# Moving small VectorE work inside the expert loops, two exponentials and one PSUM copy of a two-block transformer kernel

## What is computed

```python
def moe_ffn(tok, router_w, router_b, w1, w3, w2):
    ...
    for e in range(N_EXPERTS):                 # 16 experts, two of them chosen per token
        hid = jax.nn.silu(tok @ w1[e]) * (tok @ w3[e])
        out = out + gate[:, e:e + 1] * (hid @ w2[e])
    return out

def gla_chunk_scan(q, k, v, log_f):            # called for two directions, 8 heads
    ...
    b = jnp.cumsum(gc, axis=3)
    q_t = qc * jnp.exp(b)
    k_t = kc * jnp.exp(-b)
    ...

def dilated_window_attention(q, k, v, bias_table, window, dilation):
    ...
    m = jnp.max(s, axis=-1, keepdims=True)
    p = jnp.exp(s - m)
    ...
    o = jnp.einsum('bnqrhd,bnkrhd->bnqrhd', p, vh) / den[..., None]
```

## Time and profile before

| | us |
|---|---|
| three runs | 1763.42, 1764.65, 1765.15 |
| median | 1764.65 |
| the profiled execution, its own time | 1761.54 |
| its span in the trace | 1759.7 |
| PE busy, share of the span | 95% |
| DVE busy | 66% |
| ACT busy | 57% |
| share of PE in the chain that ended last | 80% |
| mean granted clock of TensorE | 0.988 |

### The profile page before, as it was taken

How to read it: one execution, slowest core, us unless ns; L and a number is a source line. 1 busy time by engine, 2 the same in 40 slices (tenths; PEclk the granted TensorE clock), 3 DMA queues, 4 the chain that set the end, 5 groups by cost and what they waited for, 6 DMA issues and landing times.

```text
span 1759.7 us, 30091 instructions
## 1 busy us (share of the span) xinstructions
PE 1679.4 (95%) x12246; PEld 1436.6 (82%) x12246; DVE 1154.5 (66%) x1595; ACT 1007.2 (57%) x1334; POOL 69.5 (4%) x66
## 2 busy tenths in 40 slices
PE   6999989899999989999999799999989999999898
PEld 4787666889888868889889688888869998897688
DVE  5332864789999874343465788989865677544564
ACT  4322753578888875224353678888854572453462
POOL 0000000000000110000000000000000000100100
PEclk9999999999999999999999899999999999999999
DMA  8646205899999954223574499999954443363512
GB/s 337 213 127 253 111 25 219 303 383 405 407 405 400 395 208 180 96 95 127 214 283 160 173 380 408 400 407 407 384 217 180 167 180 146 93 220 144 156 61 72
DMA packets 52556, 419.78 MB, mean 239 GB/s; under 512 B 16980, under 2 KB 18132, under 8 KB 30048
## 3 DMA queue, kind: packets, MB, share of 16 engines
q1 hardware_dynamic: 26416, 364.55, 52.6%
q0 software_dynamic: 8304, 31.64, 6.1%
q10 hardware_dynamic: 17728, 22.02, 3.7%
HBM read 398.22 MB, written 19.97 MB: 238 GB/s over the span
## 4 chain that ended last, share of the span: by engine, by line
PE 80%; DVE 8%; DMA 5%; ACT 4%; issue 3%; POOL 1%; SPq 0%; DVEq 0%; ACTq 0%; POOLq 0%
PE ps L755 47%; PE ps L900 17%; PE ps L716 4%; DMA ring<-w_all 3%; PE ps L739 2%; PE ps L909 1%; DMA y_d<-arena 1%; DVE w_lo L2314 1%; PE ps L1143 1%; PE ps L1154 1%; PE ps L1428 1%; PE ps L1169 1%; PE ps L916 1%; PE ps L762 1%; DMA arena<-y_d,tok_row 1%
## 5 line engine op out<-in xcount | busy, mean ns | idle before, releaser
L2314 DVE TENSOR_TENSOR w_lo<-ring,w_hi 128x1024 fp32r<-128x1024 f32 x384 | 452.4, 1219 | 50.8 <-ACT w_hi L1653 49.2
L1653 ACT ACTIVATE w_hi<-ring 128x1024 fp32r<-128x1024 f32 x384 | 395.7, 1056 | 106.9 <-PE ps L900 62.9
L755 PE MATMUL ps<-XT_lo,arena_r 128*128 128x256 f32 (+1 forms) x1712 | 384.6, 299 | 5.2 <-DVE ring_r L2166 3.9
L755 PEld LDWEIGHTS ps<-XT_lo,arena_r 128*128 128x128 f32 x1712 | 281.4, 189 | 21.0 <-issue 7.9
L900 PE MATMUL ps<-w_hi,x_hi 128*128 128x256 f32 (+1 forms) x768 | 250.1, 326 | 7.6 <-DVE w_lo L2314 4.8
L900 PE MATMUL ps<-w_lo,x_hi 128*128 128x256 f32 (+1 forms) x768 | 245.8, 320 | 0.0
L900 PE MATMUL ps<-w_hi,x_lo 128*128 128x256 f32 (+1 forms) x768 | 245.8, 320 | 0.0
L755 PE MATMUL ps<-arena_r 128*128 128x512 f32 (+1 forms) x656 | 230.6, 360 | 7.0 <-DVE arena_r L2486 3.7
L2166 DVE TENSOR_TENSOR ring_r<-ring,arena_r 128x1024 fp32r<-128x1024 f32 x96 | 114.0, 1222 | 108.4 <-ACT arena_r L1553 108.1
L755 PE MATMUL ps<-XT_lo,ring_r 128*128 128x256 f32 x640 | 180.9, 283 | 0.0
L900 PEld LDWEIGHTS ps<-w_hi,x_hi 128*128 128x128 f32 x768 | 147.2, 192 | 26.2 <-issue 8.9
(11 more groups left out here) (372 smaller groups left out, 2659.9 us busy)
## 6 DMA issues: line engine op xcount, KB each, us to landing
ring<-w_all SPq DMA_DIRECT2D x172, 2048.0 KB, 9.7
y_d<-arena ACTq DMA_DIRECT2D x30, 512.0 KB, 10.0
arena<-toep_d POOLq DMA_DIRECT2D x16, 384.0 KB, 12.1
arena<-rpb ACTq DMA_DIRECT2D x16, 192.0 KB, 3.8
xtok_d<-arena ACTq DMA_DIRECT2D x6, 512.0 KB, 3.2
hT<-h SPq DMA_DIRECT2D x2, 1024.0 KB, 6.1
arena<-cb_d POOLq DMA_DIRECT2D x1, 1536.0 KB, 12.0
arena<-cc_d POOLq DMA_DIRECT2D x1, 959.0 KB, 6.0
```

The lines of the kernel that those rows point to most:

```text
L755: last = nc.tensor.matmul(out, a, b, start=(first and i == 0), stop=(final and i == 2))
L1653: nc.scalar.activation(w_hi[:, q], slot(b, "p (q c) -> p q c", q=4)[:, q], ACT.Copy).then_inc(hi_rdy, 1)
L2314: nc.vector.tensor_tensor(w_lo[:, q], slot(base + n, "p (q c) -> p q c", q=4)[:, q], as_f32(w_hi[:, q]), ALU.subtract).then_inc(*split_sig ...
```

## The change

Three edits, and PE's program is left as it is. In `routed` on DVE, `weights_of_rows` becomes three functions with the same 20 instructions: `two_rows` (6 instructions) stands in turn 1 behind `gate_half` 0, `rows_taken` (6) in turn 1 ahead of `hidden_lo` 1, and `gates_taken` (8) in turn 14 ahead of `copy_rows(15)`; nothing is left behind `split(1, 0)`. On ACT, the first direction's exponentials move from step 12 to step 11; the second direction's stay in step 13. In the attention, the first copy out of PSUM moves from step 3, ahead of the exponentials of piece 3, to step 2, ahead of those of piece 2, and the two `last_split` move ahead of the exponentials of piece 1.

```diff
-                if u in (12, 13):
-                    act.wait_ge(b_rdy, u - 11)
-                    nc.scalar.activation(lf[:, u - 12], bc[:, u - 12], ACT.Exp)
-                    nc.scalar.activation(bc[:, u - 12], bc[:, u - 12], ACT.Exp, scale=-1.0).then_inc(e_rdy, 1)
+                if u in (11, 13):
+                    d = (u - 11) // 2
+                    act.wait_ge(b_rdy, d + 1)
+                    nc.scalar.activation(lf[:, d], bc[:, d], ACT.Exp)
+                    nc.scalar.activation(bc[:, d], bc[:, d], ACT.Exp, scale=-1.0).then_inc(e_rdy, 1)
...
             for i in range(len(AT_PAIRS) + 2):
-                if i >= 3:
+                if i == 1:
+                    last_split(0)
+                    last_split(1)
+                if i >= 4:
                     act.wait_ge(sx_t, AT0 + i - 2)
-                    if i >= 4:
-                        act.wait_ge(sx_o, AT0 + i - 3)
+                    act.wait_ge(sx_o, AT0 + i - 3)
+                    nc.scalar.activation(probsT2, ps[:, 4:7, :].rearrange("p b k -> p (b k)"), ACT.Copy).then_inc(sx_c, 1)
+                if i == 2:
+                    act.wait_ge(sx_t, AT0 + 1)
                     nc.scalar.activation(probsT2, ps[:, 4:7, :].rearrange("p b k -> p (b k)"), ACT.Copy).then_inc(sx_c, 1)
                 if 1 <= i < len(AT_PAIRS):
                     at_exp(i)
-                if 1 <= i < 3:
-                    last_split(i - 1)
...
-                def weights_of_rows():
+                def two_rows():
...
                     link(nc.vector.tensor_tensor(rsum, rsum, rmax, ALU.subtract))
+
+                def rows_taken():
+
                     link(nc.vector.tensor_tensor(kept, rsum, before_last, ALU.mult))
...
                     nc.vector.tensor_scalar(tok_row[:, 0:nt], rmax, -1.0, None, ALU.add)
+
+                def gates_taken():
+
                     link(nc.vector.tensor_tensor(tmp, top, gates, ALU.mult))
...
                     gate_half(e, j, 0)
+                    if first and j == 1:
+                        two_rows()
                     split(e, 2, (0, 1))
                     hidden_lo(e, 0)
                     gate_half(e, j, 1)
                     split(e, 2, (2,))
                     if begin:
                         tokens(2, 2, EXPERTS)
+                    if first and j == 1:
+                        rows_taken()
                     hidden_lo(e, 1)
                     split(e, 2, (3,))
+                    if not first and not last_e and isinstance(e, int):
+                        gates_taken()
                     if not last_e:
                         copy_rows(e + 1, 1 - j)
                         split(e + 1, 0, range(4))
-                    if begin:
-                        weights_of_rows()
```

## The result

| | before | changed |
|---|---|---|
| median of six runs, us | 1764.90 | 1753.43 |
| lowest, highest | 1761.64, 1765.81 | 1750.83, 1757.27 |
| ratio | | 0.9942 (95%: 0.9930 to 0.9954) |
| ratio, measured a second time | | 0.9951 (0.9937 to 0.9965) |
| profiled execution, us; span | 1761.54; 1759.7 | 1755.12; 1753.3 |

The change is faster by 0.58%, by 0.49% in the second measurement: 8.6 to 10.2 us. The forecast was 11.8.

What follows compares the result with a forecast made beforehand. PE is busy nearly all of the span, so only its waits and low clock can be won: 3.1 + 2.8 (experts) + 4.4 (recurrence) + 1.5 (attention) = 11.8 us, from the median 1764.65 to 1752.9 us; range 1749.0 to 1760.5.

Steps and rivals of the forecast that it cites:

- the first rival: The clock falls all the same, at remaining waits or the new 0.90; gain 6.5 us, time 1758.2 us; chance 0.10.
- the slow stretches vanish with the waits: Turn 1 of both expert layers and unit 16: low clock, twice 1.88 and 1.54, 5.3 us, goes with the waits.
- Turn 1, removal: Experts: PE's wait ahead of V and the slow V go whole, 4.17 us in layer 0, 3.7 in layer 1.
- clock term: The 5.3 us of low clock in the sum; without it the gain is 6.5 instead of 11.8 us.
- The new wait: Turn 1, layer 0: `two_rows` takes 1.28 us against 0.38 of slack, so PE waits 0.90 us.
- the experts' two terms: Net gains of the experts' edit: 3.1 us in layer 0 and 2.8 us in layer 1.
- `gates_taken` at nothing: Experts, turns 14 and 15: PE starts turn 15 about 0.5 us late, costed at nothing because DMA landings cover it.
- Recurrence: Units 14 to 16: the 2.82 us wait and 1.54 of low clock go, about 0.2 less 0.15 returns; 4.4 us gained.
- Attention: Product 0 comes 2.5 us sooner, later pieces gain 1.7 (even) or 1.1 (odd); 1.5 us taken.
- The weight stream: Rival: weight DMA bounds the expert loops, both layers give nothing; gain 5.9 us, time 1758.8 us; chance 0.12.
- The late third block: Rival: in every expert loop turn the third weight block lands late, PE waits 1.3 us; net 1784 us; chance 0.04.

Runs made afterwards that it cites:

- part_experts: The kernel before with only the experts' edit (the three functions in the experts' turns); ratio to before 0.9979, 3.7 us less.
- part_recurrence: The kernel before with only the recurrence's edit (first direction's exponentials in step 11); ratio to before 0.9978, 3.9 us less.
- part_attention: The kernel before with only the attention's edit (first copy and the two `last_split` moved); ratio to before 0.9988, 2.1 us less.
- attention_copy: The kernel before with the attention's first copy moved to step 2, the two `last_split` left where they were; ratios to before 1.0000 and 0.9996.
- idle_places: The changed kernel with `two_rows` ahead of `split(1, 1)` in turn 1, `gates_taken` ahead of `split(15, 1)` in turn 15; ratios to before 0.9927 and 0.9936.
- second_copy: The kernel of idle_places with the attention's copy of piece 1 also moved, ahead of the exponentials of piece 3; ratio to before 0.9941.

## Why the prediction was right, and where it was not

**The total** lies inside the range and goes the way that was forecast. The medians, 1753.4 for 1752.9, agree better than the gains do, 8.6 to 10.2 us for 11.8, and that closeness is luck. The range also took in the first rival (1758.2), so only the parts can decide between the two. What the waits cost was read rightly in sum. The sum was 1.6 to 3.2 us too large, most likely by what it booked for the clock.

**The step that was too large: the slow stretches vanish with the waits.** The text took 5.3 of its 11.8 us from it, twice 1.88 and 1.54. Counted over all thirteen profiles, by the granted clock of each microsecond:

| slow stretch | wait there | wait taken away |
|---|---|---|
| layer 0, V of turn 1 (359) | 3 of 6 | 0 of 7 |
| layer 0, D of turn 0 (346) | 2 of 6 | 5 of 7 |
| layer 1, V of turn 1 (1022) | 2 of 6 | 0 of 7 |
| clock lost from 285 to 372 (layer 0), us | 5.1 to 6.8, mean 5.7 | 3.4 to 6.8, mean 5.4 |
| clock lost around 965 to 1028 (layer 1), us | 6.8 in each | 5.1 to 8.5, mean 6.6 |
| unit 16 (1431) | 3 of 6 | 0 of 7 |
| last projections (1727 to 1737) | 0 of 4 | 6 of 9 |

The last row counts by the attention's edit, the ones above by that of the experts or of the recurrence. At the three places of the forecast a wait of 1.8 to 2.8 us is followed by the low clock in 8 of 18 cases, and where the wait is gone it never falls there (0 of 21). But around turn 1 of either layer what no longer falls in turn 1 falls nearby, in these profiles. Only at unit 16 is a part won on the spot: from the recurrence's first matmuls (1311.79 in the profile of before) to the start of unit 22 (1474.59), the six profiles with the wait take 161.3 to 164.0 us, mean 162.4, and the seven without it all 158.2. Of these 4.2 us, 3.1 are the wait (161.3 is the value at full clock) and 1.1 the clock.

Thirteen profiles are few, and their mean granted clocks mislead: it is 0.988 in both first profiles. But every timed run has a granted clock of its own. Span times (1 - clock) is the clock lost in that run, in us:

| kernel | runs | clock lost, mean us | less than before, us (95%) |
|---|---|---|---|
| before, all rounds | 63 | 24.6 | |
| changed, both measurements | 12 | 19.4 | 5.2 (3.5 to 6.9) |
| part_experts | 11 | 21.9 | 2.8 (1.3 to 4.2) |
| part_recurrence | 12 | 23.5 | 1.2 (-0.7 to 3.1) |
| part_attention | 12 | 23.2 | 1.5 (-0.4 to 3.3) |
| attention_copy, both | 24 | 26.2 | -1.6 (-3.0 to -0.1) |
| idle_places, both | 12 | 20.0 | 4.7 (3.0 to 6.3) |
| second_copy | 5 | 22.1 | 2.6 (1.0 to 4.1) |

So the change does take low clock away, and about as much as the 5.3 us of the forecast (5.1 in the round in which the two kernels ran side by side). But a lost us isn't a us of time everywhere: the attention's stretch takes 68.9 us with a slow stretch of 1.7 in it and 68.7 with none in the two profiles of idle_places, 69.7 and 68.6 in those of attention_copy. Among the runs of one kernel (151 runs, each against the mean of its kernel in its round) the time rises by 0.60 us for each us of clock lost. By that, an estimate, the clock gave 3.1 us where the forecast had 5.3. The means of the same runs lie 10.0 us apart, so 6.9 are left for all else. Which stretches went is not resolved, except that the experts' edit has a share.

The prediction had as its first rival that none of the low clock would go, with a chance of 0.10, and neither it nor the forecast's full 5.3 is what came. The rule that it set beside it, that the clock gate's windows run free of the kernel (the Trainium skill, "TensorE: Matmul & The Clock Gate", Part 1: The HAM clock gate), agrees with the traces: one and the same wait was followed by either level, and one kernel profiled twice had its stretches at 330 and 347 once and at 319 and 346 the other time. The error was to take one profile's coincidence of wait and clock for the full price of each wait. The 1.88 itself was also a little large: from U of turn 1 to U of turn 2 a slow stretch costs 1.6 us (21.96 for 20.33) in layer 0 and 1.5 (21.54 for 20.06) in layer 1.

Point by point:

- **Turn 1, removal.** The wait of 2.29 us went whole and V had no new one, as forecast. At full clock, from U of turn 1 to U of turn 2, it is 20.33 us before (part_attention: 352.40 to 372.73), 19.03 in the changed kernel (354.15 to 373.18) and 17.97 in idle_places: 1.30 won, 1.06 left over; the forecast had 0.90 and 0.2 coming back, 1.1. The forecast without its clock term is 4.17 - 1.88 - 1.1 = 1.2. In layer 1, 20.0 to 20.1 became 18.9, 1.2 us, for 3.7 - 1.88 - 0.9 = 0.9.
- **The new wait.** Forecast 0.90, measured 0.78, as `two_rows` has 1.30 us and the slack was 0.52 instead of 0.38. Doubling the cost added 1.31, which confirms the form of the term, cost less slack. With the clock's 1.9 taken out, the experts' two terms give 2.1 us. Measured: 3.7 by the times; by profiles 1.2 in layer 0 (315 to 650: 335.5, mean of six, and 334.3, mean of three) and 1.7 in layer 1 (993 to 1312: 317.8 and 316.1). Part of both is clock: the six lost 3.4 and 4.3 us in these stretches, the three 2.8 and 3.4, so at equal clocks some 0.7 and 0.8 are left, which is turn 1's 1.3 and 1.2 less about what the new waits at turn 15 take.
- **`gates_taken` at nothing.** Half right. PE did wait for it, 0.66 and 0.52 us, and in the first profile of the changed kernel turn 15 of layer 0 was not held by a landing, as the forecast said it would be. Still, the way out of layer 0 took no longer beyond the spread of the profiles, and when the piece was moved into idle time nothing was won there. The cover in layer 0 was real, but it lay behind turn 15, in the landings that the chain runs through. In layer 1, U of turn 14 to the first matmul of the next projection took 59.1 to 59.8 us in four profiles with it there and 58.4 in idle_places, but 60.5 in second_copy and 60.6 in the second profile of idle_places. It goes with the last block's landing, 11.5 to 12.1 us in the four, 10.9 in idle_places, 12.6 and 12.0 in the other two; but these also lost 3.4, 1.7, 5.1 and 3.4 us of clock there, and the two are not told apart.
- **Recurrence.** 4.4 forecast, 3.9 by the times and 4.2 by the profiles. No wait above 0.2 us ahead of unit 14 or 16, though neither had slack. (Unit 14 began at 1416.31, not near 1416.6 as the text worked out; the 0.1 us that PE waits there is what this leaves.)
- **Attention.** 1.5 forecast, between 1.1 and 1.7. The profiles of before and of part_attention run alike to scores 3 (1660.60 and 1660.61) and then give the bounds themselves: product 0 comes 2.51 sooner, product 1 1.28, product 2 1.96, product 4 1.65, and the last projections' first wait ends at 1722.03 instead of 1723.67, **1.64**. But both spans are 1759.7: the whole gain went to a slow stretch in the last projections (part_attention, 0.51, for 1.00 before).

```profile
1735.00:1738.00 3.00, 3.00 (x15) 3.00 (x16) 1.35 (x2) 0.00 (x0) 0.00 (x0) 0.51 0.00 0
```

  From that wait's end to the last matmul it is 32.8 to 33.2 us in the four profiles without the attention's edit, and 34.6 to 34.9 in six of the nine with it. On the average 1.2 us are given back, which is what the times of the attention's kernels (2.1, 0.0 and 0.7 us) say within their uncertainty. Over the 36 timed runs of part_attention and attention_copy the clock lost is 25.2 us, for 24.6 before, which is no difference beyond noise. Whether an earlier product 0 calls the stretch forth, or six of nine against none of four is chance, stays open; that the tail has waits of its own just ahead (0.62 and 1.19 us, in all kernels) is only an observation.
- **The other rivals.** The weight stream doesn't bound the loops: from U of turn 2 to U of turn 14, layer 0 takes 216.8 to 217.1 us in the six kernels with the experts untouched, 217.0 in the changed kernel and 217.7 in its second profile. The late third block came once: in turn 2 of layer 1 of part_experts ACT waited 2.47 us for it and PE 1.38 (that layer's loop took 219.0 us, for 217.0 to 217.7 in the other twelve profiles). It did not come in every turn.

**Budget from the profiles:** layer 0 1.2, layer 1 1.7, recurrence 4.2, attention 2.3, last projections -1.2, in all 8.2, against 8.6 and 10.2 by the times. (The attention's 2.3 is the difference of the means, 71.4 and 69.1; the pair with equal clocks gives 1.64.) At equal clocks it is 0.7, 0.8, 3.1 and 1.6, in all 6.2, where the forecast without its clock term has 6.5. So what was said of the waits is borne out in sum, and 2.4 to 4.0 us of the measured gain are left for the clock, where the forecast had 5.3 and the estimate above has 3.1.

## What to carry to other kernels

Small instructions on an engine that is not the bottleneck cost what they exceed idle time and slack at their very place: put them where the timeline shows that engine idle and not beside it; the same 1.30 us cost 0.78 in one place and nothing 6 us earlier in the turn. Don't book a low clock behind a wait as part of the wait's price on the strength of one profile. Take three or more, and count how often it follows. Above all read the granted clock of every timed run: here twelve runs against 63 showed a drop of 5.2 us that the profiles alone did not show, and the runs of one kernel among themselves showed what a lost us costs. Where a gain is smaller than one slow stretch, compare stretches between profiles with equal clocks, and then look behind the edit for where it might be given back.

## What the runs showed of the hardware

- Slow stretches come in portions: each loses 1.7 us of full clock, the longer ones 3.4 or 5.1. In thirteen profiles 19 to 26 us were lost in all. Two profiles of each don't tell before and changed kernel apart (20.9 and 25.8; 20.5 and 22.4), the timed runs do (24.6 and 19.4, means of 63 and 12).
- A lost us costs 0.60 us of time on the average of 151 runs. It depends on the place: at unit 16 one stretch costs 1.5 us (13.05 for 11.51 for the 96 matmuls), in the attention, where PE has waits of its own, 0.2 in one pair of profiles and 1.1 in another.
- They don't wander at will. They have a few places, near 28, 295, 318 or 330, 346 or 359, 970, 984, 1300, 1655, each in most profiles, and choose between neighbouring ones. In the six profiles with the experts untouched, a stretch at 318 to 320 went with one at 359 three times and with none once, and one at 329 with one at 346 twice.
- PE stood 2.09 us and went on at full clock, and at unit 16 stood 2.82 to 2.84 us six times and lost nothing three times, 1.7 once and 3.4 twice.
- The last weight block of layer 1 landed in 12.9 us in the profile of before, and in 10.9 to 12.7 in the others. The way out of the layer varies by 2 us between the profiles, more than the experts' edit gains there.
